# Experts of a hybrid decoder step: where in a block's turn its gated rows are transposed

## The reference: what is computed

```
def expert_block(args):
    xb, e = args
    return (jax.nn.silu(xb @ w1[e]) * (xb @ w3[e])) @ w2[e]
...
ys = lax.map(expert_block, (xs, block_expert)).reshape(n_slots, d)
ys = ys * slot_gate[:, None].astype(ys.dtype)
return jnp.zeros((n_tok + 1, d), t.dtype).at[slot_tok].add(ys)[:n_tok]
```

## Time and profile before

| what | value |
|---|---|
| median of 3 runs | 2430.75 us (2430.59 to 2433.07) |
| profiled execution, its own time | 2429.75 us |
| its span in the trace | 2428.0 us |
| TensorE busy, matmuls | 2214.1 us, 91% of the span |
| VectorE busy | 1283.8 us, 53% |
| ScalarE busy | 975.2 us, 40% |
| expert blocks, layer 0 and 1 | 25 and 27 |

### The profile page before, as it was taken

How to read it: one execution, slowest core, us unless ns; L and a number is a source line. 1 busy time by engine, 2 the same in 40 slices (tenths; PEclk the granted TensorE clock), 3 DMA queues, 4 the chain that set the end, 5 groups by cost and what they waited for, 6 DMA issues and landing times. The chain is left out here.

```text
span 2428.0 us, 35171 instructions
## 1 busy us (share of the span) xinstructions
PE 2214.1 (91%) x12110; PEld 1936.5 (80%) x12111; DVE 1283.8 (53%) x1938; ACT 975.2 (40%) x1509; POOL 300.6 (12%) x226
## 2 busy tenths in 40 slices
PE   7999999599999995999999999994995999999980
PEld 7999988478888883879999999983884888888860
DVE  4434443555557744426545555553865455475545
ACT  5111122345557643212444334444333445464532
POOL 0000000000111101113212222212001000010003
PEclk9999999699999997999999999997996999999995
DMA  5011131557759884541443333456325557697556
GB/s 184 31 48 53 44 111 44 199 183 299 290 201 400 314 301 122 185 158 64 125 117 83 114 126 108 125 140 225 137 78 208 194 221 276 260 335 299 212 173 238
DMA packets 212310, 426.55 MB, mean 176 GB/s; under 512 B 34800, under 2 KB 87792, under 8 KB 208880
## 3 DMA queue, kind: packets, MB, share of 16 engines
q1 hardware_dynamic: 191296, 349.90, 41.6%
q0 software_dynamic: 12704, 46.14, 5.7%
q10 hardware_dynamic: 8208, 29.13, 3.0%
HBM read 350.15 MB, written 85.48 MB: 179 GB/s over the span
## 5 line engine op out<-in xcount | busy, mean ns | idle before, releaser
L1077 DVE TENSOR_TENSOR raw_low_w<-raw_w,raw_high_w 128x2048 fp32r<-128x2048 f32 x128 | 287.1, 2284 | 25.0 <-ACT raw_high_w L1003 23.5
L1680 PE MATMUL hd_pj<-lb_xh,lr_wh 128*128 128x384 f32 (+1 forms) x768 | 270.3, 352 | 5.2 <-PEq L1338 3.5
L1680 PE MATMUL hd_pj<-lb_xh,lr_wl 128*128 128x384 f32 (+1 forms) x768 | 252.0, 328 | 0.0
L1680 PE MATMUL hd_pj<-lb_xl,lr_wh 128*128 128x384 f32 (+1 forms) x768 | 252.0, 328 | 0.0
L1003 ACT ACTIVATE raw_high_w<-raw_w 128x2048 fp32r<-128x2048 f32 x120 | 222.9, 1910 | 23.8 <-DMA raw_w<-in_expert_w 23.8
L1077 DVE TENSOR_TENSOR e_wl_w<-raw_w,e_wh_w 128x2048 fp32r<-128x2048 f32 x64 | 143.8, 2288 | 161.4 <-ACT e_wh_w L1003 161.4
L229 PE MATMUL cv_pp<-lx_xh,lx_wh 128*128 128x384 f32 (+1 forms) x576 | 189.3, 329 | 3.0 <-DVE lx_wl L420 3.0
L229 PE MATMUL cv_pp<-lx_xh,lx_wl 128*128 128x384 f32 (+1 forms) x576 | 188.3, 327 | 0.0
L229 PE MATMUL cv_pp<-lx_xl,lx_wh 128*128 128x384 f32 (+1 forms) x576 | 188.3, 327 | 0.0
L940 PE MATMUL e_py<-e_wh_w,e_hh 128*128 128x512 f32 x416 | 170.6, 410 | 15.7 <-DVE e_hl L1091 9.8
L940 PE MATMUL e_pa<-raw_high_w,e_xh 128*128 128x512 f32 x416 | 167.8, 403 | 10.0 <-DVE e_xl L1087 4.9
(11 more groups left out here) (279 smaller groups left out, 4579.3 us busy)
## 6 DMA issues: line engine op xcount, KB each, us to landing
raw_w<-in_expert_w SPq DMA_DIRECT2D x96, 2048.0 KB, 11.8
s_ys<-e_ys ACTq DMA_DIRECT2D x52, 512.0 KB, 6.2
s_ys<-e_zero SPq DMA_DIRECT2D x32, 512.0 KB
lr_wr<-in_w_heads SPq DMA_DIRECT2D x32, 512.0 KB, 5.5
mg_og<-s_og SPq DMA_DIRECT2D x24, 520.0 KB, 4.7
h<-in_conv_w_in_t SPq DMA_DIRECT2D x7, 1536.0 KB, 6.8
s_og<-hd_ob SPq DMA_DIRECT2D x16, 520.0 KB, 6.2
hd_vb<-out_o_v SPq DMA_DIRECT2D x16, 512.0 KB, 7.1
```

The lines of the kernel that those rows point to most:

```text
L1077: op = dve.tensor_tensor(wl[m][:, k, :], raw[m][:, k, :], wh[m][:, k, :].bitcast(F32), ALU.subtract)
L1680: mm = pe.matmul(pj[x % 2][:, 0:cn], w[:, q % 2, k, :], v[:, k, c0:c0 + cn], start=(k == 0 and m == 0), stop=(k == DK - 1 and m == 2))
```

## The change

The four transposes of a block's hidden rows move from the next block's turn, where they stood between up and gate, to the end of the block's own turn, behind the down product of the block before it. Those of block 0 move ahead of the loop. On ScalarE the high copy of the hidden rows moves behind the copy of the next w3, and `rows` moves behind the copy of w2; on VectorE the low part moves behind the low part of the next w3. At the end of layer 0's stage the value weights' first half is copied in two parts with the last `rows` between them. No instruction is added or taken away in work done; the diff:

```diff
--- before.py
+++ after.py
@@ -977,17 +977,17 @@
             up(0, 0)
             gate(0, 0)
             x_transposes(1)
+            hidden_transposes(0)
             last = last_block(pe)
             with pe.Fori(1, MBLK) as b:
                 with pe.If(b <= last):
                     e = expert_of(pe, b)
                     up(b, e)
-                    hidden_transposes(b - 1)
                     gate(b, e)
                     x_transposes(b + 1)
 
                     down(b - 1, expert_of(pe, b - 1))
-            hidden_transposes(last)
+                    hidden_transposes(b)
             down(last, NE - 1)
 
         @block.scalar
@@ -1033,34 +1033,35 @@
             with act.If(e_next > 0):
                 high(0, e_next, a_ok, 1)
                 high(1, e_next, b_ok, 1)
+            hidden_high(0)
             with act.Fori(1, MBLK) as b:
                 with act.If(b <= last):
                     before, e, after = (expert_of(act, b + n) for n in (-1, 0, 1))
                     silu(b)
-                    hidden_high(b - 1)
                     with act.If(after > e):
                         high(0, after, a_ok, b + 1)
                     x_high(b + 1)
                     with act.If(after > e):
                         high(1, after, b_ok, b + 1)
-                    rows(b - 1)
+                    hidden_high(b)
                     with act.If(e > before):
                         high(2, e, y_ok, b)
-            hidden_high(last)
+                    rows(b - 1)
             if R.next is None:
                 rows(last)
             else:
-                def next_high(half):
+                def next_high(half, ks):
                     act.wait_ge(R.next.ready[half], 16)
                     if half == 0:
                         act.wait_ge(lo_ok[2], NE + ONE)
-                    for k in range(DK):
+                    for k in ks:
                         act.activation(R.next.high[:, half, k], raw[half][:, k], ACT.Copy, scale=G.gcol[:, GAIN_KV, k:k + 1])\
                             .then_inc(R.next.high_ok, 1)
 
-                next_high(0)
+                next_high(0, range(DK // 2))
                 rows(last)
-                next_high(1)
+                next_high(0, range(DK // 2, DK))
+                next_high(1, range(DK))
             act.wait_ge(stored, last * 16 + 16 + ONE)
             act.sem_inc(passed_end, 1)
 
@@ -1101,19 +1102,19 @@
             with dve.If(e_next > 0):
                 low(0, e_next)
                 low(1, e_next)
+            hidden_low(0)
             with dve.Fori(1, MBLK) as b:
                 with dve.If(b <= last):
                     before, e, after = (expert_of(dve, b + n) for n in (-1, 0, 1))
-                    hidden_low(b - 1)
                     with dve.If(after > e):
                         low(0, after)
                     hidden(b)
                     x_low(b + 1)
                     with dve.If(after > e):
                         low(1, after)
+                    hidden_low(b)
                     with dve.If(e > before):
                         low(2, e)
-            hidden_low(last)
             if R.next is not None:
                 for n in range(2 * DK):
                     half, k = divmod(n, DK)
```

## The result

The changed kernel is slower: 2464.92 us (median of 4 runs, 2463.01 to 2467.94) against 2430.67 (4 runs on the same chip, 2429.87 to 2433.07), a ratio of fast runs of 1.013 with a 95% interval of 1.0115 to 1.0146 (the two medians alone give 1.0141). By the medians that is 34 us more; the forecast was 6.6 less, and the time lies far outside the range. The prediction was wrong.

A forecast was written before the change was run, and what follows sets the result against it. TensorE was taken to bound the loop, with holes only at its ends. Heads 0.8, layer 0's tail 2.5, layer 1's tail 2.5 and clock 0.8 made 6.6 us off: 2424.2 us as a median, range 2422.0 to 2428.0.

The forecast's parts named there:

- the second rival: ScalarE's loop turn at full DMA queues: 1.4 us a turn costs nine blocks 0.7 us each, 2430.5 us; 13 in 100.
- In the loop: nothing: Inside the expert loop: hidden rows always ready before what up waits for, so no gain or loss.
- Heads: Start of each layer's loop: block 0's transposes move into TensorE's 2.45 us hole; 0.8 us saved in all.
- Tail of layer 0: End of layer 0's stage: following ScalarE, VectorE's last subtraction ends at 943.5 instead of 945.98; gain 2.5 us.
- fast pitch: Layer 0's last down product: it would start near 925.4 on the old scale and stay at this pitch.
- Tail of layer 1: End of layer 1's loop: w2 copy starts 0.72 us earlier, last product at 2359.5 instead of 2362.03; gain 2.5 us.
- Clock: Layer 1's last product: a pause of about 7.2 instead of 9.77 us leaves TensorE less slow; gain 0.8 us.
- its dear case: ScalarE's loop turn at 2.3 us: 7.8 us above, about 2438.5 us; 6 in 100.

The follow-up runs named there:

- Experiment 4: Kernel before, with only TensorE's four transposes moved to the end of the block's own turn (block 0's ahead of the loop): 2430.97 us, ratio 0.9998.
- experiment 1: Changed kernel, with rows(b-1) and its store put back ahead of the w2 copy on ScalarE: 2426.46 us, ratio 0.997.
- Experiment 5: Changed kernel, with the store of the rows and its wait moved into the next turn behind silu, copy order kept: 2423.66 us, ratio 0.9951.

## Why the prediction was wrong

**The step that failed** is the price of ScalarE's turn in the second rival, "ScalarE comes late where the loads bind": "A full turn reads three expert numbers as well, which no row shows uncovered. At 1.4 us a turn". The mechanism was named, its bound was right ("decides for slower from 2.0 us a turn"; 1.3 × 9 there is 11.7, not 11.5), and the price was wrong; in the forecast's own sum it stood at nothing ("In the loop: nothing"). From the store's issue to silu it takes 593.54 − 590.15 − 0.35 = 3.0 us in the turn above; the longest wait ahead of silu is 4.9. No row shows the reads uncovered, but covered rows give their price as well: they stood in the trace of before, line 877 on ScalarE's sequencer. There they reach from 581.1 past 583.1, 2.0 us and more, so that 0.7 for an empty turn and these gave 2.7 without any run, beyond the border of 2.0. "DMA: Bandwidth & Descriptors" of the Trainium skill, Latency and other measured facts, gives a floor of some 600 ns for such a load; three of them and the empty turn are an estimate of 2.5 us, beyond that border as well. In the two turns shown the medians are 275 and 277 ns, below that floor, and the longest 0.86 and 0.67 us (over the whole run the medians are 474 and 288 ns); with the register work around them three reads take 2.4 us (591.0 to 593.4).

**How many turns.** I took nine blocks, from the waits for loads in a stretch in which the DMA engines are full. ScalarE's bare turns are 29, nearly every turn in which the expert changes (two layers with 16 experts each, the first of each ahead of the loop, make 30, and behind layer 1's last change no turn follows), whether the queues are full or not. By the rival's own sum a turn of 3.0 us is 1.59 + 0.60 + 3.0 − 2.8 = 2.4 us late; what TensorE loses is 39.7 / 29 = 1.4 us, since part of the delay meets slack. The argument against the rival, that late copies let other loads finish sooner, came to little: waits for w1 and w3 loads fell from 23.8 to 18.0 us.

**"In the loop: nothing"** is wrong in its second half. It holds that the hidden rows are always ready before what up waits for, and they are (600.39 against 600.99). But I let that mean that waiting at the transposes costs no more than waiting at up. In a stalled turn the transposes stop TensorE at the end of its turn, its own branch and read come bare behind them (1.65 us instead of 0.36), and some of these stops cost clock. What I put at nothing measured 39.7 us. Experiment 4 shows that without ScalarE's delay none of it occurs.

**The terms of the sum.** *Heads*: the pause is 1.88 us instead of 2.45, with the transposes inside; up starts 490.24 − 486.96 = 3.28 us behind hidden, as before (3.29), so 0.36 us a layer are saved: right. *Tail of layer 0*: 2.7 against 2.5, right along ScalarE's path. TensorE's had one wait that I missed: the last down product waited 1.80 us for rows(23), since py exists once. That it started 2.40 us behind the loop's last product, where 2.5 was forecast for another reason, is luck. Nor did it stay at the fast pitch, a sign that I had named: its starts took 7.02 us (948.17 to 955.19). Both stayed nearly hidden: ScalarE's way out of the loop took until 952.86, and it waited 0.29 us for the product. *Tail of layer 1*: a pause of 7.18 us, forecast 7.2; right. *Clock*: wrong, zero. From first to last start the product took 8.10 us behind a pause of 7.2, and 7.92 behind one of 9.8. The straight line between two points was no rule: behind the same pause of 1.8 us layer 0's last product took 7.02 us here and 5.47 in experiment 1. "TensorE: Matmul & The Clock Gate" of the Trainium skill, Part 1, says that the number of slow matmuls varies from run to run, and a term of 0 by it would have been nearer; these two traces agree as far as they go. The four were meant to bring 6.6 us; what the changed kernel's rows show of them is 0.7 + 2.7 + 2.4 = 5.8. The 7.2 of experiment 1 (4.9 to 10 by its interval) don't confirm the sum: its w2 copy stands behind the rows again, so layer 1's last product waits 9.0 us and not 7.2. Experiment 5 has all four and brings 11.4 (8.3 to 15.6), more than they explain; where the rest comes from is open.

**The forecast's chances.** A rival with 19 in 100 came in, with a price beyond both of its cases; the range stopped at 2428 because its dear case had only 6.

## What to carry to other kernels

A loop with run-time branches has a turn of its own on every engine, and the turn's length is in the trace, among the sequencer's rows, also where work covers it. Before you move the last instruction of a turn, ask whether the sequencer must wait for it: a long copy at the end covers the next turn's reads, while a store that waits for the copy ahead of it lays them bare. Keep such a wait away from the end (move the store into the next turn, or a long copy behind it), and look for it on each engine; moving it was tried here on ScalarE alone.

## What was not expected of the hardware

Stops of the same length left the clock alone or not. These are the first 5.7 us of up in three stalled turns of the changed kernel, up's instructions alone (length, then TensorE's busy time and count; the clock is the number ahead of the DMA share):

```profile
602.78:608.48 5.70, 5.70 (x24) 4.42 (x24) 0.00 (x0) 1.00 0.92 301
697.47:703.17 5.70, 5.70 (x19) 4.58 (x20) 0.00 (x0) 0.74 0.93 297
774.51:780.21 5.70, 5.70 (x18) 4.52 (x19) 0.00 (x0) 0.70 0.99 342
```

The first follows pauses of 1.58 and 0.99 us at full clock (2.4 GHz). The second follows shorter ones, these:

```profile
695.77 0.66 PE L965 MATMUL e_ph<-ident,e_hid 128*128 128x128 f32 x4 [1.22 <-DVE e_hid L1084]
...
697.47 0.79 PE L940 MATMUL e_pa<-raw_high_w,e_xh 128*128 128x512 f32 x1 [1.04 <-DVE e_xl L1088]
```

and runs at 0.74 in the mean, a part of it at the lower level (1.2 GHz), with 19 matmuls in place of 24. The third, behind pauses of 1.31 and 1.03 us, runs at 0.70, and so do up's first 5.7 us from 2069.20 and from 2334.60, with 18 matmuls each. At these clocks the four lose 1.5 and three times 1.7 us, some 6.6 of the loop's 11.9 us of longer busy time. I did not find what decides between the two cases.
